# One-hot factors of a gate matrix: two engines write them token by token with scalar compares, in straight code

## The chip, the cores and the metric

The kernel runs on one core of one Trainium2 chip, as one launch. The metric is the device time of that launch in microseconds (us), the median of three runs. Engines are named as the profile names them: PE multiplies matrices, DVE, ACT and POOL work on 128-partition tiles, SP issues the transfers.

## What is computed

Two blocks run one after the other on 256 tokens of width 1024. The first has two layers, each a bank of five mixers and then a feed-forward over product keys (PEER), and the change lies in that feed-forward. The second is a recurrent layer and a gated delta layer, which the change does not touch. The reference of the feed-forward, cut to what matters:

```python
sc = einsum('bshjc,hjkc->bshjk', q, subkeys)            # 8 heads, 2 halves, 128 keys
top_s, top_i = top_k(sc, 16)
best, ci = top_k(top_s[..., 0, :, None] + top_s[..., 1, None, :], 16)
idx = i1 * 128 + i2                                      # i1, i2: keys picked in the two halves
g = softmax(best)
act = gelu(einsum('ckd,cd->ck', u_tab[idx], x))
out = einsum('ck,ckd->cd', g * act, v_tab[idx])
```

Each token picks 8 x 16 = 128 of 128 x 128 experts, each with a gate g. The kernel does not gather the experts. It goes through all of them, 128 at a time, and multiplies by a gate matrix G that holds, for each token, the gate of each expert and zero where it was not picked.

## The kernel before

The loop over two layers (`nc.Fori(0, LAYERS)`) holds one program per engine, tied together by semaphores alone: there is no scheduler, and each engine runs its rows in the order in which they are written. The feed-forward of a layer has four stages.

1. Queries and key scores on PE, top 16 on DVE, and then the slots: per token 128 numbers i1, 128 numbers i2 and 128 gates, which PE transposes (L537) and ACT copies to `slot` (L741), so that a partition is a slot and a column a token.
2. The gate matrix. For each token t the matrix is a product on PE of two 128 x 128 factors: `ha` has in row p a one at column i1 of slot p, times the gate of slot p; `hb` has in row p a one at column i2. Tokens are taken four at a time, 64 groups per layer. DVE makes each factor of a group with one TENSOR_TENSOR over 128 x 512 that compares `iota` (a row 0 to 127) with `slot`, both broadcast (`one_hot`, L1097). POOL multiplies `ha` by the gates in place (`gate_rows`, L841). PE multiplies (`gate_products`, L547), four products into a bank, banks 0 and 1 in turn, and ACT copies the bank to `G` (L748).
3. The experts: 256 chunks from memory through the ring `weight_ring`, split in two parts by ACT (L755) and DVE (L1129), multiplied by PE (L570 and L582).
4. The sum, turned back and added to the token stream.

Around the change the order is set by these semaphores. `first_hot` says that DVE has written a group of `ha`, `first_gated` that POOL has gated it, `second_hot` that `hb` is there, `g_ready` that PE has multiplied a group and `g_kept` that ACT has copied it. There are four buffers for `ha` and two for `hb`, all inside the weight ring (from column WSIZE + D), so SP holds back the expert load number E_HOT and all behind it until the last group is multiplied (L329). Loads 0 and 1 are let through before. PE, DVE and ACT all start stage 3 only behind the last `g_kept` (PE at L559). PE, POOL and DVE run the groups in hardware loops of four groups a turn, ACT in one of two a turn, with the token's column as a register address; the last four groups of DVE are written out.

Of the kernel before, what the change touches and what calls it, by code (L numbers as in the profile page):

```python
# [9 lines left out]
ALU = mybir.AluOpType  # L10
# [82 lines left out]
E_HOT = 2  # L93
assert (N_ALL + E_HOT) % WSLOTS == 2

# [51 lines left out]
def first_block(nc, ctx, mem_, ins):  # L147
# [72 lines left out]
    ha = hot(4, 4, P)  # L220
    hb = hot(2, 4, P)
    GROUPS = T // 4
    ROUND = 4
# [61 lines left out]
    with nc.Fori(0, LAYERS) as l:  # L285
        with nc.Block() as block:

            @block.sync
            def _(sp):
# [36 lines left out]
                for k in range(WSLOTS):  # L326
                    sp.wait_ge(s("w_used"), N_ALL + k - WSLOTS + 1)
                    if k == E_HOT:
                        sp.wait_ge(s("g_ready"), 4 + GROUPS)  # L329
                    sp.dma_start(wring[:, (N_ALL + k) % WSLOTS, 0:D], d_e[l, k]).then_inc(s(f"w_loaded{(N_ALL + k) % WSLOTS}"), 16)  # L330
# [6 lines left out]
            def _(pe):  # L337
# [203 lines left out]
                def gate_products(g, count):  # L541

                    pe.wait_ge(s("first_gated"), count)
                    pe.wait_ge(s("second_hot"), count)
                    pe.wait_ge(s("g_kept"), count)
                    for j in range(4):
                        last = nc.tensor.matmul(nc_ps[g % 2][:, j * P:(j + 1) * P], ha[:, g % 4, j], hb[:, g % 2, j], start=True, stop=True)  # L547
                    last.then_inc(s("g_ready"), 1)

                with pe.Fori(0, GROUPS // ROUND) as i:  # L550
                    for g in range(ROUND):
                        gate_products(g, i * ROUND + (g + 1))


                pe.wait_ge(s("g_kept"), 2 + T // 4)
# [53 lines left out]
            def _(act):  # L609
# [118 lines left out]
                for m in range(2 * PH):  # L728
                    act.wait_ge(s("w_used"), N_WQ + m + 1)
                    nc.scalar.copy(query[:, m], nc_ps[m % 4][:, 0:T]).then_inc(s("query_kept"), 1)  # L730
                    if (m >= 2 and m % 2 == 0) or m == 2 * PH - 1:
# [4 lines left out]
                        nc.scalar.copy(score[:, h % 4], nc_ps[4 + h % 4][:, :].rearrange("p (a c) -> p a c", a=2 * NT)).then_inc(s("score_kept"), 1)  # L736
                act.wait_ge(s("best_shifted"), 1)
# [5 lines left out]
                act.wait_ge(s("slots_kept"), 1)  # L743
                act.sem_inc(s("g_kept"), 2)
                with act.Fori(0, T // 8) as i:
                    for g in range(2):
                        act.wait_ge(s("g_ready"), i * 2 + (g + 5))
                        nc.scalar.copy(G[:, bass.ds(i * 8 + 4 * g, 4)], nc_ps[g][:, :].rearrange("p (a c) -> p a c", a=4)).then_inc(s("g_kept"), 1)  # L748
# [33 lines left out]
            def _(pool):  # L782
# [56 lines left out]
                def gate_rows(g, position, count):  # L839
                    pool.wait_ge(s("first_hot"), count)  # L840
                    nc.gpsimd.tensor_tensor(ha[:, g % 4], ha[:, g % 4], slot[:, 2, bass.ds(position, 4)].unsqueeze(2).broadcast_to([P, 4, P]),  # L841
                                            ALU.mult).then_inc(s("first_gated"), 1)

                with pool.Fori(0, GROUPS // ROUND) as i:
                    for g in range(ROUND):
                        gate_rows(g, i * (4 * ROUND) + 4 * g, i * ROUND + (g + 1))

            @block.vector
            def _(dve):
# [245 lines left out]
                def one_hot(out, half, position, ready):  # L1095

                    nc.vector.tensor_tensor(out, iota.unsqueeze(1).broadcast_to([P, 4, P]),  # L1097
                                            slot[:, half, bass.ds(position, 4)].unsqueeze(2).broadcast_to([P, 4, P]),
                                            ALU.is_equal).then_inc(s(ready), 1)

                dve.sem_inc(s("g_ready"), 4)
                one_hot(ha[:, 0], 0, 0, "first_hot")
                with dve.Fori(0, GROUPS // ROUND - 1) as i:
                    for g in range(ROUND):
                        dve.wait_ge(s("g_ready"), i * ROUND + (g + 2))
# [982 lines left out]
```

## Time and profile before

| what | us |
|---|---|
| median of three runs | 2940.0 (2939.86 to 2942.03) |
| span of the profiled execution | 2947.2 |
| PE busy | 2511.8 (85%) |
| DVE busy | 2067.6 (70%) |
| ACT busy | 1024.6 (35%) |
| POOL busy | 677.2 (23%) |
| L1097, the one-hots on DVE, both layers | 262.3 |
| L841, the gating on POOL, both layers | 169.2 |

The profiled execution is one of its own, and of its time only the span is known. It lies 7.2 us, 0.24%, above the median of the timed runs. The busy figures are sums over the whole span, so that an engine that is fully busy for a short stage and idle for the rest looks idle here; such a stage is read from the rows of its own stretch.

### The profile page before, as it was taken

To read this page: it belongs to the slowest core of one execution; us is meant where nothing else is said; L and a number is where in the kernel's file an instruction comes from. 1 tells how busy PE (TensorE), PEld (TensorE's weight loads), DVE (VectorE), ACT (ScalarE), POOL (GpSimd) and SP (SyncE) were. 2 spreads that over 40 slices of the span, in tenths; PEclk is the share of its full clock that TensorE was granted. 3 is DMA by queue.
4 is the path that set the end of the run, shared out by engine and by line. 5 is a ranking of instruction groups with operands and counts; after the bars stand their busy time and mean duration, and the time that the engine had idled before them with its cause. 6 is when DMAs were issued, how large, how long until landed. Compare 5 with 4: busy or idle time off the path is not lost. (4 is left out here: it accounts for less than half of the span.)

```text
span 2947.2 us, 44691 instructions
## 1 busy us (share of the span) xinstructions
PE 2511.8 (85%) x15512; PEld 2266.9 (77%) x15512; DVE 2067.6 (70%) x3346; ACT 1024.6 (35%) x1572; POOL 677.2 (23%) x548
## 2 busy tenths in 40 slices
PE   7859456999999999987593579999999999768898
PEld 7738346899999999877373468999999998758897
DVE  7585999666666666685769996666666665749652
ACT  4221122444444444342211224444444444444321
POOL 5571256000000000055712560000000000516340
PEclk9769778999999999987697789999999999889898
DMA  5424100555555555453241005555555554424201
GB/s 189 142 72 157 51 0 0 178 186 187 188 187 185 185 186 187 140 188 127 74 161 43 0 0 189 189 186 186 189 187 185 185 185 140 141 87 146 76 1 36
DMA packets 107647, 392.07 MB, mean 133 GB/s; under 512 B 11952, under 2 KB 13360, under 8 KB 107184
## 3 DMA queue, kind: packets, MB, share of 16 engines
q1 hardware_dynamic: 107568, 391.02, 39.4%
q8 instruction: 49, 0.80, 0.1%
q14 instruction: 30, 0.25, 0.0%
HBM read 389.93 MB, written 1.05 MB: 133 GB/s over the span
## 5 line engine op out<-in xcount | busy, mean ns | idle before, releaser
L570 PEld LDWEIGHTS bank<-x_parts,chunk_parts 128*128 128x128 f32 x6144 | 772.0, 192 | 23.1 <-DVE chunk_parts L1129 3.5
L570 PE MATMUL bank<-x_parts,chunk_parts 128*128 128x256 f32 x6144 | 778.5, 283 | 2.5 <-DVE chunk_parts L1129 2.5
L1129 DVE TENSOR_TENSOR chunk_parts<-weight_ring,chunk_parts 128x1024 fp32r<-128x1024 f32 x512 | 625.6, 1223 | 196.3 <-ACT chunk_parts L755 196.3
L582 PE MATMUL bank<-chunk_parts,weight_parts 128*128 128x512 f32 x3072 | 744.7, 391 | 0.6 <-DVE chunk_parts L1129 0.6
L755 ACT CAST chunk_parts<-weight_ring 128x1024 fp32r<-128x1024 f32 x512 | 535.7, 1047 | 359.3 <-PE bank L582 359.3
L582 PEld LDWEIGHTS bank<-chunk_parts,weight_parts 128*128 128x128 f32 x3072 | 560.7, 188 | 106.8 <-issue 0.9
L1121 DVE TENSOR_TENSOR work<-work,big 128x256 f32<-128x256 f32 x256 | 163.0, 637 | 278.7 <-ACT work L759 278.7
L1097 DVE TENSOR_TENSOR weight_ring<-constants,work 128x512 f32<-128x512 f32 x256 | 262.3, 1101 | 4.1 <-ACT work L741 4.1
L759 ACT ACTIVATE work<-bank 128x256 f32<-128x256 f32 x256 | 98.3, 384 | 466.8 <-PE bank L570 466.8
L547 PE MATMUL bank<-weight_ring 128*128 128x128 f32 x1024 | 184.1, 337 | 83.9 <-issue 74.8
L547 PEld LDWEIGHTS bank<-weight_ring 128*128 128x128 f32 x1024 | 160.8, 240 | 107.5 <-issue 98.9
L841 POOL TENSOR_TENSOR weight_ring<-weight_ring,work 128x512 f32<-128x512 f32 x128 | 169.2, 1322 | 119.1 <-DVE weight_ring L1097 119.1
L1411 PE MATMUL bank<-x_parts,chunk_parts 128*128 128x256 f32 x1152 | 153.0, 297 | 25.5 <-POOL chunk_parts L1401 25.5
L785 POOL MEMSET big<- 128x572 f32 x2 | 1.2, 576 | 740.9 <-issue 734.9
L1411 PEld LDWEIGHTS bank<-x_parts,chunk_parts 128*128 128x128 f32 x1152 | 150.2, 205 | 27.5 <-POOL chunk_parts L1401 12.6
L1317 POOL MEMSET big<- 128x24 f32 x1 | 0.1, 123 | 732.3 <-issue 732.3
L748 ACT COPY big<-bank 128x512 f32 x128 | 75.0, 586 | 192.4 <-PE bank L547 192.4
L1401 POOL TENSOR_TENSOR chunk_parts<-weight_ring,chunk_parts 128x1024 fp32r<-128x1024 f32 x48 | 123.3, 2580 | 76.7 <-ACT chunk_parts L1395 76.7
L256 POOL TENSOR_TENSOR big<-big 128x512 f32<-128x512 f32 (+4 forms) x190 | 124.0, 653 | 14.9
L527 PE MATMUL bank<-big,weight_ring 128*128 128x256 f32 x512 | 117.1, 388 | 5.9 <-DVE big L860 5.9
L407 PE MATMUL bank<-x_parts,chunk_parts 128*128 128x256 f32 x768 | 104.8, 299 | 17.1 <-issue 12.0
L253 POOL TENSOR_TENSOR big<-big 128x1024 f32<-128x1024 f32 x38 | 93.1, 2450 | 105.2 <-DMA big<-in_ada 105.2
(355 smaller groups left out, 2812.6 us busy)
## 6 DMA issues: line engine op xcount, KB each, us to landing
weight_ring<-in_experts SPq DMA_DIRECT2D x512, 512.0 KB, 3.3
big<-in_ada SPq DMA_DIRECT2D x48, 512.0 KB, 4.3
weight_ring<-in_w_in SPq DMA_DIRECT2D x40, 512.0 KB, 4.6
weight_ring<-in_wq SPq DMA_DIRECT2D x32, 512.0 KB, 3.2
weight_ring<-in_gdn_in SPq DMA_DIRECT2D x32, 512.0 KB, 3.3
weight_ring<-in_w_out SPq DMA_DIRECT2D x16, 640.0 KB, 4.0
weight_ring<-in_lru_in SPq DMA_DIRECT2D x16, 512.0 KB, 3.3
weight_ring<-in_w_kv SPq DMA_DIRECT2D x8, 512.0 KB, 4.4
```

The source lines that it names most:

```text
L256: link(ops.tensor_tensor(w_[:, 0:width], w_[:, 0:width], w_[:, width:2 * width], ALU.add))
L527: last = nc.tensor.matmul(nc_ps[m % 4][:, 0:T], wt[:, k], xn[:, k], start=(k == 0), stop=(k == KD - 1))
L547: last = nc.tensor.matmul(nc_ps[g % 2][:, j * P:(j + 1) * P], ha[:, g % 4, j], hb[:, g % 2, j], start=True, stop=True)
L570: last = nc.tensor.matmul(nc_ps[2 + n % 2][:, 0:T], a[:, j * P:(j + 1) * P], xr[:, x, j], start=(j == 0 and a is hi and x == 0), stop=(j = ...
L582: last = nc.tensor.matmul(nc_ps[4 + 2 * tt + c][:, 0:512], wr[:, x, n % 2, tt * P:(tt + 1) * P], v[:, c * 512:(c + 1) * 512], start=False, ...
L755: nc.scalar.copy(split[:, k % SPLITS, 0], wring[:, slot_, 0:D]).then_inc(s("hi_done"), 1)
L841: nc.gpsimd.tensor_tensor(ha[:, g % 4], ha[:, g % 4], slot[:, 2, bass.ds(position, 4)].unsqueeze(2).broadcast_to([P, 4, P]), ALU.mult).the ...
L1097: nc.vector.tensor_tensor(out, iota.unsqueeze(1).broadcast_to([P, 4, P]), slot[:, half, bass.ds(position, 4)].unsqueeze(2).broadcast_to([P ...
L1121: nc.vector.tensor_tensor(wgt[:, n % 2], act_e[:, n % 2], G[:, :, bass.ds(tile, 1)].squeeze(2), ALU.mult).then_inc(s("w_full"), 1)
L1129: nc.vector.tensor_tensor(split[:, k % SPLITS, 1], wring[:, (N_ALL + k) % WSLOTS, 0:D], split[:, k % SPLITS, 0].bitcast(F32), ALU.subtract ...
L1401: nc.gpsimd.tensor_tensor(split[:, n % SPLITS, 1], ring[n % R2], split[:, n % SPLITS, 0].bitcast(F32), ALU.subtract).then_inc(s("lo_done"), 1)
L1411: last = nc.tensor.matmul(out, split[:, n % SPLITS, a, k * P:(k + 1) * P], xr[:, x, k], start=(k == 0 and a == 0 and x == 0), stop=(k == K ...
```

## The change

DVE no longer writes `ha`. It writes `hb` alone, with four TENSOR_SCALAR of 128 x 128 per group, one per token, each comparing iota with one column of `slot` as a scalar per partition. Its iota is a copy in PSUM bank 3, which ACT makes once per layer, between the last key scores and the Exp of the gates. POOL writes `ha` from nothing, also with four TENSOR_SCALAR of 128 x 128 per group, which compare iota (in SBUF) with one column of `slot` and multiply by the gate's column. `first_hot` is gone. Both factors have three buffers (HOTS) in place of four and two, in the same space. All loops over groups are written out, so addresses and waits are constants.

```diff
--- before.py
+++ after.py
@@ -91,6 +91,7 @@
 
 NE = 2 * NK
 E_HOT = 2
+HOTS = 3
 assert (N_ALL + E_HOT) % WSLOTS == 2
 
 
@@ -217,10 +218,10 @@
     wgt = w(2, T)
     hot = Region(mem_["wring_"], WSLOTS * WSIZE + P * 2)
     hot.at = WSIZE + D
-    ha = hot(4, 4, P)
-    hb = hot(2, 4, P)
+    ha = hot(HOTS, 4, P)
+    hb = hot(HOTS, 4, P)
     GROUPS = T // 4
-    ROUND = 4
+    iota_ps = nc_ps[3][:, 0:P]
     out_e = big[:, 0:D]
     G = big[:, :].rearrange("p (t k) -> p t k", t=T)
 
@@ -326,7 +327,7 @@
                 for k in range(WSLOTS):
                     sp.wait_ge(s("w_used"), N_ALL + k - WSLOTS + 1)
                     if k == E_HOT:
-                        sp.wait_ge(s("g_ready"), 4 + GROUPS)
+                        sp.wait_ge(s("g_ready"), GROUPS)
                     sp.dma_start(wring[:, (N_ALL + k) % WSLOTS, 0:D], d_e[l, k]).then_inc(s(f"w_loaded{(N_ALL + k) % WSLOTS}"), 16)
                 with sp.Fori(0, NE // WSLOTS - 1) as i:
                     for e in range(WSLOTS):
@@ -538,21 +539,19 @@
                     last.then_inc(s("slots_turned"), 1)
 
 
-                def gate_products(g, count):
-
-                    pe.wait_ge(s("first_gated"), count)
-                    pe.wait_ge(s("second_hot"), count)
-                    pe.wait_ge(s("g_kept"), count)
+                for g in range(GROUPS):
+                    pe.wait_ge(s("first_gated"), g + 1)
+                    pe.wait_ge(s("second_hot"), g + 1)
+                    if g == 0:
+                        pe.wait_ge(s("slots_kept"), 1)
+                    if g >= 2:
+                        pe.wait_ge(s("g_kept"), g - 1)
                     for j in range(4):
-                        last = nc.tensor.matmul(nc_ps[g % 2][:, j * P:(j + 1) * P], ha[:, g % 4, j], hb[:, g % 2, j], start=True, stop=True)
+                        last = nc.tensor.matmul(nc_ps[g % 2][:, j * P:(j + 1) * P], ha[:, g % HOTS, j], hb[:, g % HOTS, j], start=True, stop=True)
                     last.then_inc(s("g_ready"), 1)
 
-                with pe.Fori(0, GROUPS // ROUND) as i:
-                    for g in range(ROUND):
-                        gate_products(g, i * ROUND + (g + 1))
-
-
-                pe.wait_ge(s("g_kept"), 2 + T // 4)
+
+                pe.wait_ge(s("g_kept"), GROUPS)
                 pe.wait_ge(s("zeros"), 1)
                 for tt in range(NT):
                     for c in range(2):
@@ -734,18 +733,17 @@
                         if h >= 4:
                             act.wait_ge(s("score_used"), h - 3)
                         nc.scalar.copy(score[:, h % 4], nc_ps[4 + h % 4][:, :].rearrange("p (a c) -> p a c", a=2 * NT)).then_inc(s("score_kept"), 1)
+                act.wait_ge(s("query_kept"), 2 * PH)
+                nc.scalar.copy(iota_ps, iota).then_inc(s("iota_there"), 1)
                 act.wait_ge(s("best_shifted"), 1)
                 nc.scalar.activation(ex, ex, ACT.Exp).then_inc(s("best_exp"), 1)
                 act.wait_ge(s("slots_turned"), NT)
                 for j in range(3):
                     last = nc.scalar.copy(slot[:, j], nc_ps[j][:, 0:T])
                 last.then_inc(s("slots_kept"), 1)
-                act.wait_ge(s("slots_kept"), 1)
-                act.sem_inc(s("g_kept"), 2)
-                with act.Fori(0, T // 8) as i:
-                    for g in range(2):
-                        act.wait_ge(s("g_ready"), i * 2 + (g + 5))
-                        nc.scalar.copy(G[:, bass.ds(i * 8 + 4 * g, 4)], nc_ps[g][:, :].rearrange("p (a c) -> p a c", a=4)).then_inc(s("g_kept"), 1)
+                for g in range(GROUPS):
+                    act.wait_ge(s("g_ready"), g + 1)
+                    nc.scalar.copy(G[:, 4 * g:4 * g + 4], nc_ps[g % 2][:, :].rearrange("p (a c) -> p a c", a=4)).then_inc(s("g_kept"), 1)
 
 
                 def high(k, slot_, loaded, free):
@@ -836,14 +834,15 @@
                                             ALU.mult).then_inc(s("hit_keyed"), 1)
 
 
-                def gate_rows(g, position, count):
-                    pool.wait_ge(s("first_hot"), count)
-                    nc.gpsimd.tensor_tensor(ha[:, g % 4], ha[:, g % 4], slot[:, 2, bass.ds(position, 4)].unsqueeze(2).broadcast_to([P, 4, P]),
-                                            ALU.mult).then_inc(s("first_gated"), 1)
-
-                with pool.Fori(0, GROUPS // ROUND) as i:
-                    for g in range(ROUND):
-                        gate_rows(g, i * (4 * ROUND) + 4 * g, i * ROUND + (g + 1))
+                pool.wait_ge(s("slots_kept"), 1)
+                pool.wait_ge(s("w_used"), N_ALL)
+                for g in range(GROUPS):
+                    if g >= HOTS:
+                        pool.wait_ge(s("g_ready"), g - HOTS + 1)
+                    for j in range(4):
+                        t = 4 * g + j
+                        last = nc.gpsimd.tensor_scalar(ha[:, g % HOTS, j], iota, slot[:, 0, t:t + 1], slot[:, 2, t:t + 1], ALU.is_equal, ALU.mult)
+                    last.then_inc(s("first_gated"), 1)
 
             @block.vector
             def _(dve):
@@ -1092,27 +1091,15 @@
                 dve.wait_ge(s("slots_kept"), 1)
                 dve.wait_ge(s("w_used"), N_ALL)
 
-                def one_hot(out, half, position, ready):
-
-                    nc.vector.tensor_tensor(out, iota.unsqueeze(1).broadcast_to([P, 4, P]),
-                                            slot[:, half, bass.ds(position, 4)].unsqueeze(2).broadcast_to([P, 4, P]),
-                                            ALU.is_equal).then_inc(s(ready), 1)
-
-                dve.sem_inc(s("g_ready"), 4)
-                one_hot(ha[:, 0], 0, 0, "first_hot")
-                with dve.Fori(0, GROUPS // ROUND - 1) as i:
-                    for g in range(ROUND):
-                        dve.wait_ge(s("g_ready"), i * ROUND + (g + 2))
-                        one_hot(ha[:, (g + 1) % 4], 0, i * (4 * ROUND) + 4 * (g + 1), "first_hot")
-                        dve.wait_ge(s("g_ready"), i * ROUND + (g + 3))
-                        one_hot(hb[:, g % 2], 1, i * (4 * ROUND) + 4 * g, "second_hot")
-                for g in range(GROUPS - ROUND, GROUPS):
-                    if g + 1 < GROUPS:
-                        dve.wait_ge(s("g_ready"), g + 2)
-                        one_hot(ha[:, (g + 1) % 4], 0, 4 * (g + 1), "first_hot")
-                    dve.wait_ge(s("g_ready"), g + 3)
-                    one_hot(hb[:, g % 2], 1, 4 * g, "second_hot")
-                dve.wait_ge(s("g_kept"), 2 + T // 4)
+                dve.wait_ge(s("iota_there"), 1)
+                for g in range(GROUPS):
+                    if g >= HOTS:
+                        dve.wait_ge(s("g_ready"), g - HOTS + 1)
+                    for j in range(4):
+                        t = 4 * g + j
+                        last = nc.vector.tensor_scalar(hb[:, g % HOTS, j], iota_ps, slot[:, 1, t:t + 1], None, ALU.is_equal)
+                    last.then_inc(s("second_hot"), 1)
+                dve.wait_ge(s("g_kept"), GROUPS)
```

Here is how the rows of two engines stand. First DVE from the last reduction of the slots to the first split of stage 3. `weight_ring` is where `ha` and `hb` lie, `work` holds `slot`, `constants` holds iota, `bank` is PSUM, and `m_` stands before each semaphore's name. Before, within the loop:

```order
363 L1087 TENSOR_REDUCE big<-big 128x128 [waits m_hit_keyed]
364 L1097 TENSOR_TENSOR weight_ring<-constants,work 128x512 [waits m_w_used,m_slots_ready,m_slots_kept]
365 L1103 UNCONDITIONAL_BRANCH
366 L1103 ISA
367 L1097 ISA [waits m_g_ready]
368 L1097 TENSOR_TENSOR weight_ring<-constants,work 128x512
369 L1107 REGISTER_ALU
370 L1097 ISA [waits m_g_ready]
371 L1097 TENSOR_TENSOR weight_ring<-constants,work 128x512
```

And with the change:

```order
363 L1086 TENSOR_REDUCE big<-big 128x128 [waits m_hit_keyed]
364 L1100 TENSOR_SCALAR weight_ring<-bank,work 128x128 [waits m_w_used,m_iota_there,m_slots_kept,m_slots_ready]
365 L1100 TENSOR_SCALAR weight_ring<-bank,work 128x128 x11
366 L1100 TENSOR_SCALAR weight_ring<-bank,work 128x128 [waits m_g_ready]
367 L1100 TENSOR_SCALAR weight_ring<-bank,work 128x128 x3
```

Three groups (12 instructions) run before the first wait for PE, and then one wait stands before each group of four.

Second, POOL after the last multiplication of the slots' stage. Before:

```order
164 L835 TENSOR_TENSOR big<-big 128x2048 [waits m_hit_ready] x3
165 L844 UNCONDITIONAL_BRANCH
166 L844 ISA
167 L841 ISA [waits m_first_hot]
168 L841 TENSOR_TENSOR weight_ring<-weight_ring,work 128x512
169 L840 REGISTER_ALU
```

And with the change:

```order
164 L833 TENSOR_TENSOR big<-big 128x2048 [waits m_hit_ready] x3
165 L844 TENSOR_SCALAR weight_ring<-constants,work 128x128 [waits m_w_used,m_slots_kept]
166 L844 TENSOR_SCALAR weight_ring<-constants,work 128x128 x11
167 L844 TENSOR_SCALAR weight_ring<-constants,work 128x128 [waits m_g_ready]
168 L844 TENSOR_SCALAR weight_ring<-constants,work 128x128 x3
```

POOL no longer waits for DVE. It waits for ACT's copy of the slots, and then for PE alone.

## Rows read from the trace of the kernel before

**Rows 1.** The page: busy time, share of the span and instructions of each engine.
```profile
PE 2511.8 (85%) x15512; PEld 2266.9 (77%) x15512; DVE 2067.6 (70%) x3346; ACT 1024.6 (35%) x1572; POOL 677.2 (23%) x548
```

**Rows 2.** Windows, both gate stages: busy us (instructions) of each engine, PEclk, DMA.
```profile
core 0: us, PE busy (x) PEld busy (x) DVE busy (x) ACT busy (x) POOL busy (x), PEclk, DMA share, GB/s
388.50:522.00 133.50, 91.85 (x512) 80.23 (x512) 131.15 (x128) 36.93 (x63) 84.60 (x64) 0.82 0.00 0
1638.50:1771.00 132.50, 92.20 (x512) 80.53 (x512) 131.16 (x128) 36.94 (x63) 84.59 (x64) 0.82 0.00 0
```

**Rows 3.** Timeline, start of both gate stages: start, us, what [idle before <-releaser].
```profile
387.49 0.92 ACT L741 COPY work<-bank 128x256 f32<-128x256 f32 x3 [31.61 <-PE bank L537]
388.55 4.19 DVE L1097 TENSOR_TENSOR weight_ring<-constants,work 128x512 f32<-128x512 f32 x4 [2.05 <-ACT work L741]
389.44 2.75 POOL L841 TENSOR_TENSOR weight_ring<-weight_ring,work 128x512 f32<-128x512 f32 x2 [14.45 <-DVE weight_ring L1097]
...
1637.52 0.92 ACT L741 COPY work<-bank 128x256 f32<-128x256 f32 x3 [31.61 <-PE bank L537]
```

**Rows 4.** Timeline, inside the first gate stage.
```profile
439.75 16.46 DVE L1097 TENSOR_TENSOR weight_ring<-constants,work 128x512 f32<-128x512 f32 x16
...
446.17 1.30 POOL L841 TENSOR_TENSOR weight_ring<-weight_ring,work 128x512 f32<-128x512 f32 x1 [0.74 <-DVE weight_ring L1097]
...
446.68 1.87 PE L547 MATMUL bank<-weight_ring 128*128 128x128 f32 x8 [0.92 <-issue]
448.20 1.33 POOL L841 TENSOR_TENSOR weight_ring<-weight_ring,work 128x512 f32<-128x512 f32 x1 [0.72 <-DVE weight_ring L1097]
...
448.55 1.52 DVE L1097 TENSOR_TENSOR weight_ring<-constants,work 128x512 f32<-128x512 f32 x1
...
450.00 0.68 DVE L1097 TENSOR_TENSOR weight_ring<-constants,work 128x512 f32<-128x512 f32 x1
...
450.73 0.59 ACT L748 COPY big<-bank 128x512 f32 x1 [1.46 <-PE bank L547]
```

**Rows 5.** Timeline, end of both gate stages.
```profile
522.71 1.04 PE L559 MATMUL bank<-constants,zeros 128*128 128x512 bf16 x4 [0.77 <-ACT big L748]
...
1767.86 1.33 POOL L841 TENSOR_TENSOR weight_ring<-weight_ring,work 128x512 f32<-128x512 f32 x1 [0.72 <-DVE weight_ring L1097]
...
1769.83 1.13 PE L547 MATMUL bank<-weight_ring 128*128 128x128 f32 x8 [0.32 <-issue]
1771.10 0.59 ACT L748 COPY big<-bank 128x512 f32 x1 [0.86 <-PE bank L547]
...
1771.74 0.61 PE L559 MATMUL bank<-constants,zeros 128*128 128x512 bf16 x2 [0.77 <-ACT big L748]
```

**Rows 6.** Line L1097 on DVE: ns min/median/max, first and last start us, forms.
```profile
L1097 DVE TENSOR_TENSOR weight_ring<-constants,work x256: 676/1106/1530, 388.5 to 1768.2; 128x512 f32<-128x512 f32 x128
```

**Rows 7.** Timeline, DVE in the delta layer: 16 scalar instructions reading PSUM.
```profile
2780.78 4.23 DVE L1843 TENSOR_SCALAR big<-bank,work 128x128 f32<-128x128 f32 x16
```

**Rows 8.** POOL's groups by shape: busy us, mean ns.
```profile
L256 POOL TENSOR_TENSOR big<-big 128x128 f32<-128x128 f32 x38 | 19.6, 515 | 3.0
...
L258 POOL TENSOR_TENSOR big<-big 128x16 f32<-128x16 f32 x38 | 9.3, 244 | 3.0
...
L796 POOL COPY big<-big 128x512 f32<-128x512 f32 x2 | 1.2, 620 | 4.4 <-ACT big L658 4.4
...
L801 POOL COPY big<-big 64x256 f32<-64x256 f32 x2 | 0.8, 392 | 0.1
...
L1317 POOL MEMSET big<- 128x24 f32 x1 | 0.1, 123 | 732.3 <-issue 732.3
```

**Rows 9.** Timeline, POOL: two copies in a row, no wait between them.
```profile
42.35 0.39 POOL L801 COPY big<-big 64x256 f32<-64x256 f32 x1
42.79 0.40 POOL L802 COPY big<-big 64x256 f32<-64x256 f32 x1
```

## The prediction

> **What bounds the kernel now.** I read the page first. PE is busy for 85% of the span and DVE for 70% [rows 1], which says little about a stage that fills 9% of it. So I read the windows of the two gate stages [rows 2]. In 133.5 us DVE is busy for 131.15, ACT for 37, POOL for 85 and PE for 92. DVE is the bound there, and nothing else is near. The DMA share is 0.00, since the expert loads wait for the stage's end, so no transfer can be the bound inside it.
>
> Next, the pace. In the timeline DVE does 16 instructions in 16.46 us without a gap [rows 4], two per group, so a group takes 2.06 us, and 64 groups take 131.7. The two are far from equal. The one that starts at 450.00 has POOL idle beside it and takes 0.68 us; the one at 448.55 runs beside POOL's multiplication (448.20 to 449.53), takes 1.52, and the next starts only 1.45 later [rows 4]. All 256 lie between 676 and 1530 ns [rows 6]. The inference is that DVE's compare, with two inputs in SBUF, loses about 0.8 us per group to POOL.
>
> Last, the edges of the stage. It begins when ACT has copied the slots (387.49 + 0.92 = 388.41, and 1638.44 in the second layer) [rows 3] and ends when PE starts L559 (522.71 and 1771.74) [rows 5]. So it is 134.3 us long in the first layer and 133.3 in the second. All engines stand at both edges, so a microsecond saved inside is a microsecond of the kernel, twice. The rest of the program is the same, so the whole change is in these 267.6 us.
>
> **The change part by part.** With P the pace of a group, the new stage is: 0.15 us from the slots to the first compare (388.41 to 388.55 [rows 3]), then 64 P until the last factor is there, 0.1 until PE starts, and from there to L559 what rows 5 show, 1771.74 - 1769.83 = 1.9. So it is 64 P + 2.2 us, and today's pace is matched at P = (133.8 - 2.2) / 64 = 2.06. P is the largest of four costs.
>
> DVE. 256 wide compares leave the program, and per group four TENSOR_SCALAR of 128 x 128 come, with iota in PSUM and the scalar in `work`. The trace has just this form: 16 of them take 4.23 us, 0.26 each from start to start [rows 7]. A group costs 4 x 0.26 = 1.06 us, half of now. The compares of `ha` leave DVE altogether.
>
> PE. The same 256 products per layer. They keep PE busy for 91.85 us [rows 2], 1.44 us per group, because the granted clock is 0.82 of full, changing between its two levels, 2.4 and 1.2 GHz: a group takes 1.13 us at the higher [rows 5] and 1.87 where much of it fell to the lower [rows 4]. PE's floor is 1.13 if the clock is full all through, and 1.44 as it is granted now. Above a pace of 1.44, three buffers take up a slow group.
>
> ACT. 64 copies of 0.59 us [rows 5] per layer, as before. Two banks go round: product 1.13 to 1.87, copy 0.59 and two handovers of some 0.15 come to 2.0 to 2.8 us per two groups, 1.0 to 1.4 per group, no more than PE. The new copy of iota to PSUM is one small instruction per layer and stands before the Exp. ACT sat idle for 31.6 us before it copied the slots [rows 3], which covers it; without this cover it would cost less than the 0.59 of a copy four times as wide. It waits only for queries that ACT itself copied, so nothing queues up behind it.
>
> POOL. It did one multiplication per group and now does four TENSOR_SCALAR, each with a compare, a product and two scalars per partition. The trace has no such instruction on POOL. Call X its time from start to start, so that P = 4 X. Bound below: a copy reads one tensor and writes one. Two in a row start 0.44 us apart at 256 elements [rows 9]. From 392 ns at 256 to 620 at 512 elements [rows 8] an element costs 0.89 ns, so a copy of 128 would take 0.44 - 0.11 = 0.32. A compare with scalars is not cheaper than a copy, except that start-to-start times may overlap, and I keep 0.28 as the lower end. Bound above: I take the TENSOR_TENSOR of 128 x 128, 515 ns [rows 8], which reads twice as much, and beyond it the case of the rivals. The value I take is nearest to the copy, plus the fetch of the scalars. What a read costs POOL shows between a write alone, 123 ns (memset, 24 elements), and a short read and write, 244 ns (16 elements) [rows 8]: 0.12 us. With one such fetch, X = 0.32 + 0.12 = 0.44 and P = 1.76. No row of the trace gives the second arithmetic operation a cost, and I take none.
>
> Loops. 57 ns register steps and branches go, but they are hidden under DVE's instructions, as DVE has no gap [rows 4]. Straight code has more instructions to fetch. The unrolled parts of the same program run without a gap of the kind in L1843's sixteen [rows 7]; nothing is charged, and a microsecond or two per layer is within the range. The waits: POOL may be three groups ahead of PE, so its wait for group g - 3 is over long before (1.76 + 1.2 + 0.3 us of work against 5.3 us of lead). SP's wait for the last group ends with the stage, as now, and the loads behind it move with it.
>
> **The sum.** POOL sets the pace: 64 x 1.76 + 2.2 = 114.8 us per layer. That is 19.5 less in the first and 18.5 less in the second, 38.0 together. The profiled execution goes from 2947.2 to 2909.2. It lies 7.2 above the median, which I carry over: **2902 us**. PE, at 1.44 of 1.76, is next.
>
> **The rivals.** A measurement of this kernel can tell about 0.2%, 5.9 us, from no change; that is X within 0.012 of 0.514.
>
> *POOL is cheaper, PE is the bound.* If X is 0.36 or less, PE's clock decides. For it speaks that both inputs of the work are small; against it, that the copy alone already costs 0.32. At 1.44 the stage is 94.4 us, 78.8 less in all: 2861. At a full clock (1.13, X under 0.28) it would be 74.5 us: 2821.
>
> *Each scalar is a fetch of its own: slower.* The place is POOL's instruction, before its stream starts. Two fetches of 0.12 give X = 0.32 + 0.24 = 0.56 and P = 2.24, a stage of 145.6 us, 23.6 more in all: 2964. It decides from X = 0.514 upwards. For it: the short instructions on POOL all look like fixed cost, 244 ns for 16 elements [rows 8]. Against: the addresses of both scalars are known at once and may be fetched together. The Trainium skill has a rule for it (GPSIMD Engine Reference, Performance pitfalls for Q7 kernels): a small read command costs about 102 cycles and does not overlap with the one before. By its figure at 1.2 GHz, an estimate of 85 ns each, X would be 0.49 and the time 2928; no row here shows such a command by itself. A compare that costs more per element than a copy would lead to the same place: 0.9 ns more for each of 128 elements is another 0.12.
>
> *The scalars cost about what the split saves.* X within 0.012 of 0.514, which is also the TENSOR_TENSOR's 515 ns: no change, 2940.
>
> *DVE and POOL still get in each other's way.* The wide compares lose some 0.8 us per group beside POOL [rows 4]. If the narrow ones exclude POOL's, a group takes 4 x (0.26 + 0.44) = 2.8 us, and the time is 2940 + 2 x 181.4 - 267.6 = 3035. Rows 7 say nothing about it, as POOL stood still there. Against it: the iota that DVE reads is not in SBUF, so only one operand, the scalar, comes from there. The Trainium skill (SBUF — State Buffer, Who interferes with whom) says that a DVE instruction with at most one SBUF input and outside the 2-port modes does not contend with GpSimd. The trace agrees in the other half, that two SBUF inputs do (1.52 us against 0.68); the half that counts here no row shows.
>
> **How the numbers follow.** POOL sets the pace with X from 0.36 to 0.50: 0.46. PE is the bound: 0.22. No change: 0.07. Slower through the fetches or the compare: 0.21. Contention: 0.04. So faster 0.68, same 0.07, slower 0.25. The likeliest case's own range is X from 0.36 to 0.50, 64 x 1.44 + 2.2 = 94.4 to 64 x 2.0 + 2.2 = 130.2 us per layer, 2861 to 2933. To leave out no more than 2 in 10, the range goes down to where PE has a clock somewhat better than now (P about 1.32, 86.7 us, 2846) and up to X = 0.59 (153.2 us, 2979).
>
> **What the new profile would show.** DVE's instructions near 0.26 us from start to start, and DVE idle, waiting for PE, for about 40% of the stage. POOL without a gap, four instructions in 1.76 us. PE waiting for POOL before each group, and no POOL waiting for DVE. The stage's start and its end 115 us apart. The forecast is wrong if POOL waits for PE (then PE was the bound and X is small), if four POOL instructions take more than 2.06 us, if DVE's take more than 0.26 only while POOL runs, or if the time outside the two stages moves.

## The result: 140 us slower

The changed kernel takes 3080.2 us (median of four runs, 3074.4 to 3085.4) against 2939.9 for the kernel before. The ratio is 1.0475, with a 95% interval from 1.0459 to 1.0492. I had forecast 2902, with a range from 2846 to 2979.

The page of the changed kernel, its share of busy time (as rows 1 before) and the group that answers to L841 and L1097:

```profile
PE 2590.3 (84%) x15510; PEld 2332.1 (76%) x15512; DVE 1947.7 (63%) x3602; ACT 1024.7 (33%) x1574; POOL 903.1 (29%) x932
...
L844 POOL TENSOR_SCALAR weight_ring<-constants,work 128x128 f32<-128x128 f32 x512 | 396.0, 791 | 27.1 <-ACT work L742 27.1
```

POOL's 512 instructions take 396.0 us in all. POOL is busy for only 29% of the span, and yet it is the engine that sets the time, because all of these lie in two stages in which everything waits for it. The windows of the two stages, as rows 2 showed them before:

```profile
core 0: us, PE busy (x) PEld busy (x) DVE busy (x) ACT busy (x) POOL busy (x), PEclk, DMA share, GB/s
388.30:589.00 200.70, 132.81 (x512) 113.93 (x512) 71.84 (x256) 37.29 (x65) 198.00 (x256) 0.50 0.00 0
1703.00:1904.00 201.00, 132.75 (x512) 113.93 (x512) 71.85 (x256) 37.59 (x66) 198.00 (x256) 0.50 0.00 0
```

POOL is busy for 198.0 of 200.7 us. DVE went from 131 to 72 us of busy time, as intended, and now idles. PE is granted 0.50 of its clock throughout, 1.2 GHz, against 0.82 before, and does the same 512 records. The timeline of a stretch inside, and the edges of both stages (start us, us, engine, line; in brackets the idle time before):

```profile
387.42 0.92 ACT L742 COPY work<-bank 128x256 f32<-128x256 f32 x3 [31.61 <-PE bank L538]
...
439.50 8.52 POOL L844 TENSOR_SCALAR weight_ring<-constants,work 128x128 f32<-128x128 f32 x11
...
441.12 2.08 PE L550 MATMUL bank<-weight_ring 128*128 128x128 f32 x8 [1.02 <-POOL weight_ring L844]
443.23 0.58 ACT L746 COPY big<-bank 128x512 f32<-128x512 f32 x1 [2.52 <-PE bank L550]
443.23 1.13 DVE L1100 TENSOR_SCALAR weight_ring<-bank,work 128x128 f32<-128x128 f32 x4 [1.97 <-PE bank L550]
444.21 2.07 PE L550 MATMUL bank<-weight_ring 128*128 128x128 f32 x8 [1.01 <-POOL weight_ring L844]
...
589.65 1.49 PE L558 MATMUL bank<-constants,zeros 128*128 128x512 bf16 x3 [1.08 <-ACT big L746]
...
1702.47 0.92 ACT L742 COPY work<-bank 128x256 f32<-128x256 f32 x3 [31.61 <-PE bank L538]
...
1904.70 1.49 PE L558 MATMUL bank<-constants,zeros 128*128 128x512 bf16 x3 [1.08 <-ACT big L746]
```

Eleven POOL instructions take 8.52 us without a gap, so one starts (8.52 - 0.79) / 10 = 0.773 us after the other, and a group takes 3.09 us. DVE's four take 1.13 us and then wait 1.97 for PE to free a buffer. PE waits 1.0 us for POOL before each group. The stage is 589.65 - 388.34 = 201.3 us long, and as long in the second layer (1904.70 - 1703.39). Against 134.3 and 133.3 before, that is 135.0 us more. The spans differ by 3081.2 - 2947.2 = 134.0. So the whole loss is in the two stages; the medians differ by 140.3, since the profiled execution of before lay 7 us above its median and this one 1 us above its own.

### The profile page after: what moved, and what is told of

Same layout as the page of the kernel before. It is cut to its first block and busy times, and to the rows that moved or that the text cites. A ratio compares the mean times of both kernels' runs of the same rounds, so it can differ in the third digit from the quotient of the medians.

```text
span 3081.2 us, 43977 instructions
## 1 busy us (share of the span) xinstructions
PE 2590.3 (84%) x15510; PEld 2332.1 (76%) x15512; DVE 1947.7 (63%) x3602; ACT 1024.7 (33%) x1574; POOL 903.1 (29%) x932
## 5 line engine op out<-in xcount | busy, mean ns | idle before, releaser
L844 POOL TENSOR_SCALAR weight_ring<-constants,work 128x128 f32<-128x128 f32 x512 | 396.0, 791 | 27.1 <-ACT work L742 27.1
L550 PE MATMUL bank<-weight_ring 128*128 128x128 f32 x1024 | 265.6, 441 | 136.8 <-POOL weight_ring L844 128.3
L550 PEld LDWEIGHTS bank<-weight_ring 128*128 128x128 f32 x1024 | 227.9, 328 | 174.7 <-POOL weight_ring L844 174.7
L1100 DVE TENSOR_SCALAR weight_ring<-bank,work 128x128 f32<-128x128 f32 x512 | 143.7, 344 | 244.4 <-PE bank L550 240.4
L746 ACT COPY big<-bank 128x512 f32<-128x512 f32 x128 | 74.9, 585 | 326.8 <-PE bank L550 326.8
```

Of the source, the lines that this page charges most:

```text
L844: last = nc.gpsimd.tensor_scalar(ha[:, g % HOTS, j], iota, slot[:, 0, t:t + 1], slot[:, 2, t:t + 1], ALU.is_equal, ALU.mult)
L1100: last = nc.vector.tensor_scalar(hb[:, g % HOTS, j], iota_ps, slot[:, 1, t:t + 1], None, ALU.is_equal)
```

## The experiments

After the result the question was what makes POOL's instruction 0.773 us long, where I had taken 0.44. Three theories: each **scalar** costs a fixed fetch; the **arithmetic** costs per element; or DVE beside it causes **contention**. Beside them stood the parts of the change that I had costed at nothing. Each ratio below is against runs of the kernel before that were timed along with the variant (medians 2943.2 and 2942.8 us). The two tails were run once each, for the lengths of their instructions alone.

**Forms of the instruction, measured by themselves.** A tail is code behind the last layer, in which nothing else runs. Parts of it (`...` marks what is left out here):

```diff
+            for i in range(6):
+                g.tensor_copy(new(), iota)
...
+            for i in range(6):
+                g.tensor_scalar(new(), iota, s0, s1, ALU.mult, ALU.add)
+            for i in range(6):
+                g.tensor_scalar(new(), iota, s0, s1, ALU.is_equal, ALU.mult)
...
+            for i in range(24):
+                g.tensor_scalar(new(), iota, s0, s1, ALU.is_equal, ALU.mult)
+        @block.vector
+        def _(dve):
+            for i in range(64):
+                nc.vector.tensor_scalar(new(), m["ps"][3][:, 0:P], s0, None, ALU.is_equal)
```

> The kernel before, with a tail behind its last layer, in which nothing else runs, that does six to 24 POOL instructions of each form in a row, each to a place of its own, and then some of DVE. It is for the time from start to start of one instruction; the kernel's time grows by the tail and says nothing. The changed kernel showed 0.773 us for POOL's compare-and-multiply of 128 x 128 with two scalars from memory. Theory of the fetch (each scalar costs a fixed read, the stream runs like a copy): a copy 0.3, immediates in place of the scalars 0.3 to 0.35, one scalar 0.55, two 0.77 whatever the operation; 384 elements with two scalars 0.77 + 0.23 = 1.0; 32 elements 0.69. Theory of the element (the arithmetic costs per element, the scalars nothing): immediates 0.77 as with scalars, one operation clearly under two, 384 elements about 2.0, 32 elements about 0.35. Theory of contention (DVE beside it slows POOL): 0.45 alone in every form, and 0.77 only in the block where DVE runs beside it reading PSUM. In the block where DVE reads iota from SBUF instead, all theories expect both engines slower than alone, if the two ports matter. DVE alone from SBUF: about 0.19 to 0.20 from start to start against 0.26 from PSUM.

The lines of the tail, one form each (ns min/median/max of one, start of the first and the last). L1982 is a copy; L1986 an equality with an immediate, L1990 with one scalar; L1992 multiply and add with two immediates, L1994 equality and multiply with two immediates; L1996 and L1998 the same pairs with two scalars; L2000 and L2002 are L1998 at 32 and 384 elements:

```profile
L1982 POOL COPY big<-constants x6: 290/292/293, 2942.7 to 2943.9; 128x128 f32<-128x128 f32 x6
...
L1986 POOL TENSOR_SCALAR big<-constants x6: 529/532/543, 2947.2 to 2949.7; 128x128 f32<-128x128 f32 x6
...
L1990 POOL TENSOR_SCALAR big<-constants x6: 616/618/619, 2953.7 to 2956.6; 128x128 f32<-128x128 f32 x6
L1992 POOL TENSOR_SCALAR big<-constants x6: 318/320/323, 2957.2 to 2958.5; 128x128 f32<-128x128 f32 x6
L1994 POOL TENSOR_SCALAR big<-constants x6: 667/668/672, 2958.7 to 2961.8; 128x128 f32<-128x128 f32 x6
L1996 POOL TENSOR_SCALAR big<-constants x6: 471/482/486, 2962.4 to 2964.6; 128x128 f32<-128x128 f32 x6
L1998 POOL TENSOR_SCALAR big<-constants x6: 831/834/841, 2965.0 to 2968.9; 128x128 f32<-128x128 f32 x6
L2000 POOL TENSOR_SCALAR big<-constants x6: 521/525/528, 2969.6 to 2971.9; 128x32 f32<-128x32 f32 x6
L2002 POOL TENSOR_SCALAR big<-constants x6: 1703/1708/1714, 2972.3 to 2980.4; 128x384 f32<-128x384 f32 x6
```

Three readings. First, a scalar costs 618 - 532 = 86 ns, and two cost 834 - 668 = 166 in one pair and 482 - 320 = 162 in the other: two cost twice what one does, 0.083 us each, as if each were fetched by itself. Second, with two immediates multiply-add takes 320 ns, hardly more than a copy's 292, and equality-multiply 668. The pair of operations is worth 0.35 us at 128 elements, with the scalars the same. From start to start, taken from the trace, the same four forms (L1992, L1994, L1996, L1998) lie 0.26, 0.61, 0.43 and 0.77 us apart, with the same differences to 0.01 us, so these are not an effect of how the profile ends an instruction. Third, it grows with the width: from 128 to 384 elements equality-multiply gains 874 ns, 3.4 per element, where rows 8 gave 0.89 for a copy. Neither of the first two theories holds alone: above a copy's 0.24 us from start to start lie 0.54, of which the two scalars are 0.17 and the choice of operations 0.35; the rest, about 0.03, is what multiply-add takes above a copy.

And the block with DVE beside it (L2016 POOL, L2020 DVE from PSUM; L2026 POOL, L2030 DVE from SBUF; L2026 stands twice, the second time for the window in which DVE ran, 3018.1 to 3032.0 us), then DVE alone from SBUF with one operation (L2036), with two (L2038) and from PSUM with two (L2040):

```profile
L2016 POOL TENSOR_SCALAR big<-constants x24: 787/808/825, 2999.2 to 3016.9; 128x128 f32<-128x128 f32 x24
L2020 DVE TENSOR_SCALAR big<-bank,constants x64: 337/339/350, 2999.1 to 3015.4; 128x128 f32<-128x128 f32 x64
L2026 POOL TENSOR_SCALAR big<-constants x24: 787/908/1026, 3018.1 to 3038.1; 128x128 f32<-128x128 f32 x24
L2026 POOL TENSOR_SCALAR big<-constants x16: 843/910/1026, 3018.1 to 3031.8; 128x128 f32<-128x128 f32 x16
L2030 DVE TENSOR_SCALAR big<-constants x64: 271/281/396, 3018.1 to 3032.0; 128x128 f32<-128x128 f32 x64
L2036 DVE TENSOR_SCALAR big<-constants x16: 280/280/286, 3039.2 to 3042.1; 128x128 f32<-128x128 f32 x16
L2038 DVE TENSOR_SCALAR big<-constants x16: 333/336/342, 3042.3 to 3046.2; 128x128 f32<-128x128 f32 x16
L2040 DVE TENSOR_SCALAR big<-bank,constants x16: 396/396/399, 3046.4 to 3051.2; 128x128 f32<-128x128 f32 x16
```

From start to start POOL takes (3016.9 - 2999.2) / 23 = 0.77 us with DVE beside it reading PSUM, and (2968.9 - 2965.0) / 5 = 0.78 alone. The contention theory falls. With iota in SBUF, POOL's time rises to 20.0 / 23 = 0.87 and DVE's from 2.9 / 15 = 0.19 to 13.9 / 63 = 0.22. But the 0.87 mixes two stretches: as long as DVE ran, POOL's instructions started (3031.8 - 3018.1) / 15 = 0.91 us apart, and behind it 0.77 again. So beside such a DVE an instruction of POOL costs 0.14 us more.

**Straight code alone.** The kernel before, with its loops written out:

```diff
-                with pool.Fori(0, GROUPS // ROUND) as i:
-                    for g in range(ROUND):
-                        gate_rows(g, i * (4 * ROUND) + 4 * g, i * ROUND + (g + 1))
+                for g in range(GROUPS):
+                    gate_rows(g, 4 * g, g + 1)
```

(and so on PE, ACT and DVE).

> The kernel before with the loops over groups of PE, ACT, POOL and DVE written out, nothing else changed: the part of the change that is only straight code. Theory that POOL's new instruction costs all: no change, ratio 1.000, the stage stays at 133 to 134 us. Rival, that straight code itself costs (instruction fetches): the stage grows by up to the 68 us per layer that the change lost.

Measured: 2942.1 us, ratio 0.9994, interval 0.9984 to 1.0003. In its profile the two stages are 134.3 and 133.2 us long, as before. Straight code is neither the loss nor a gain.

**Which pairs are slow.** A second tail, with other pairs of operations, all with two scalars from memory:

> The kernel before with a second tail behind its last layer: POOL's TENSOR_SCALAR of 128 x 128 with two scalars from memory and other pairs of operations, six of each. Measured before: multiply then add 0.44 us from start to start, compare then multiply 0.78, a single multiply 0.58. If comparing is what is slow, all pairs without a compare take 0.44 (multiply-multiply, multiply-subtract, add-multiply, subtract-multiply, max-multiply) and equal-add and greater-multiply 0.78. If instead one pair alone, multiply-add, runs on a quick path and all others go through a general one, every other pair takes about 0.78, and at 384 elements multiply-multiply takes 1.64 as compare-multiply did, against about 0.8 for multiply-add. Output in bf16 in place of fp32: no change in either case.

L1980 is multiply-multiply, L1982 multiply-subtract, L1984 add-multiply, L1988 equality-add, L1992 max-multiply; L1996 is multiply-multiply at 384 elements:

```profile
L1980 POOL TENSOR_SCALAR big<-constants x6: 447/447/451, 2944.7 to 2946.9; 128x128 f32<-128x128 f32 x6
L1982 POOL TENSOR_SCALAR big<-constants x6: 792/792/816, 2947.3 to 2951.2; 128x128 f32<-128x128 f32 x6
L1984 POOL TENSOR_SCALAR big<-constants x6: 447/447/448, 2952.0 to 2954.1; 128x128 f32<-128x128 f32 x6
...
L1988 POOL TENSOR_SCALAR big<-constants x6: 791/791/816, 2959.2 to 2963.1; 128x128 f32<-128x128 f32 x6
...
L1992 POOL TENSOR_SCALAR big<-constants x6: 787/788/794, 2968.5 to 2972.4; 128x128 f32<-128x128 f32 x6
...
L1996 POOL TENSOR_SCALAR big<-constants x6: 660/660/661, 2977.0 to 2980.2; 128x384 f32<-128x384 f32 x6
```

Both guesses miss. The quick ones are pairs of multiply and add; a subtraction is as slow as a compare, at 792 ns, and the two pairs not shown (subtract-multiply, greater-multiply) take 792 and 791. What the edge is made of can't be seen from here; it may be a general routine behind a few special ones, which was not tested. At 384 elements multiply-multiply takes 660 ns, 0.83 per element more than at 128, where equality-multiply had 3.4. The output in bf16 took 791 ns as well. The profile's length of one form differs a little from place to place (834 ns in the first tail, 791 in the changed kernel); from start to start it is 0.77 us in both.

**The changed kernel with a quick pair.** One edit. The first factor is then no one-hot, so the gate matrix, and what comes behind it, holds other values; the work is the same in number and size.

```diff
-                        last = nc.gpsimd.tensor_scalar(ha[:, g % HOTS, j], iota, slot[:, 0, t:t + 1], slot[:, 2, t:t + 1], ALU.is_equal, ALU.mult)
+                        last = nc.gpsimd.tensor_scalar(ha[:, g % HOTS, j], iota, slot[:, 0, t:t + 1], slot[:, 2, t:t + 1], ALU.mult, ALU.add)
```

> The changed kernel, but POOL's instruction multiplies by its first scalar and adds its second in place of comparing and multiplying: same width, same two scalars from memory, another pair of operations. The first factor is then no one-hot, so the gate matrix and all behind it hold other values. In the tail measured before, this form took 0.44 us from start to start against 0.78. If the pair of operations is what the forecast of 0.44 us lacked, POOL has 1.76 us per group, the stage is 64 x 1.76 + 2.2 = 115 us as forecast, and the time 2940 - 38 = 2902, perhaps 5 more or less. If something else in the stage held the changed kernel (the waits, straight code, PE at its lower level with 2.07 us per group), the time stays at 2940 or above.

Measured: 2901.1 us, ratio 0.9862 (0.9843 to 0.9880). The windows from 400 to 480 us, and POOL's and DVE's groups in them:

```profile
400.00:480.00 80.00, 53.84 (x373) 45.00 (x373) 52.79 (x188) 27.50 (x47) 80.00 (x188) 1.00 0.00 1
...
L844 POOL TENSOR_SCALAR weight_ring<-constants,work 128x128 f32<-128x128 f32 x188 | 80.6, 443 | 0.0
L1100 DVE TENSOR_SCALAR weight_ring<-bank,work 128x128 f32<-128x128 f32 x188 | 52.9, 344 | 27.7 <-PE bank L550 27.7
```

188 of POOL's instructions in 80 us are 0.43 us each and 1.70 per group. Everything else in the stage is as the change has it: the waits, straight code, three buffers, DVE reading PSUM. With the instruction at about the length of the forecast, the kernel runs at about the time of the forecast. One price carries the error.

**DVE alone, from PSUM and from SBUF.** POOL is taken out, and DVE writes both factors; in the second kernel `iota` stands in both of its rows for `iota_ps`, and ACT's copy of iota is gone. PE no longer waits for `first_gated`. The lines added for `ha`:

```diff
+                    for j in range(0, 4):
+                        t = 4 * g + j
+                        nc.vector.tensor_scalar(ha[:, g % HOTS, j], iota_ps, slot[:, 0, t:t + 1], slot[:, 2, t:t + 1], ALU.is_equal, ALU.mult)
```

> DVE writes both factors as in the run with iota in SBUF, but reads iota from PSUM as the change does. In the tail DVE took 0.26 us for one operation and 0.32 for two with two scalars, both from PSUM, so 4 x 0.26 + 4 x 0.32 = 2.32 us per group, a stage of about 151 us and a time of about 2940 + 2 x 151 - 268 = 2974. If PSUM cost nothing, it would be 2912 as with SBUF.

> The changed kernel with POOL out of the stage: DVE writes both factors, eight narrow instructions per group, with iota read from SBUF. If the narrow form from SBUF takes 0.19 to 0.20 us from start to start (by the 341 ns that 256 elements from SBUF and 128 from PSUM both take), the pace is 1.55 to 1.6 and the time about 2880. If it takes 0.26 as from PSUM, the pace is 2.08 and the time 2940 to 2945. PE's clock could hold either at 2.07 per group.

From PSUM 2977.5 us (two runs; 1.0121, 1.0089 to 1.0153), close to the 2974 expected; from SBUF 2911.9 (0.9895, 0.9878 to 0.9911). The second was expected near 2880: the pace is 4 x 0.19 for `hb` and 4 x 0.26 for `ha`, 1.81 us, because the second operation and its scalar cost DVE another 0.06 us each, which L2038 against L2036 shows and which I had not known then. Reading iota from SBUF makes DVE's instruction shorter by 0.06 us; the change paid that for freedom from POOL. And DVE alone, without POOL's help, is 1.0% faster than the kernel before.

**The change with iota in SBUF.**

```diff
-                        last = nc.vector.tensor_scalar(hb[:, g % HOTS, j], iota_ps, slot[:, 1, t:t + 1], None, ALU.is_equal)
+                        last = nc.vector.tensor_scalar(hb[:, g % HOTS, j], iota, slot[:, 1, t:t + 1], None, ALU.is_equal)
```

> The changed kernel with DVE's iota in SBUF, which lets DVE use both ports. In the tail POOL's compare-and-multiply took 0.87 us from start to start while DVE's narrow compares ran without pause beside it, and 0.77 alone. Here DVE is busy for only a quarter of the time, so if the ports matter in proportion POOL goes to 0.79 to 0.80 and the time to 3085 to 3095. If they do not matter, 3080.

Measured: 3095.6 us (two runs; 1.0522, 1.0497 to 1.0548), at the upper end of what was expected. POOL's mean went from 791 to 820 ns, and its group from 3.09 to 3.22 us (PE starts groups at 439.43, 442.65 and 445.88). So the copy in PSUM was right for this division of the work: by the two ratios, 1.0522 and 1.0475, it is worth about 14 us. The two stages of the profile, 209.3 and 209.4 us against 201.3, give 16. The group grew by 0.13 us, about what one of its four POOL instructions costs more beside DVE in the tail (0.14).

**The work divided evenly.** POOL writes the first factor of two tokens in four, DVE that of the others and all second factors:

```diff
-                    for j in range(4):
+                    for j in range(2):
                         t = 4 * g + j
                         last = nc.gpsimd.tensor_scalar(ha[:, g % HOTS, j], iota, slot[:, 0, t:t + 1], slot[:, 2, t:t + 1], ALU.is_equal, ALU.mult)
...
+                    for j in range(2, 4):
+                        t = 4 * g + j
+                        nc.vector.tensor_scalar(ha[:, g % HOTS, j], iota_ps, slot[:, 0, t:t + 1], slot[:, 2, t:t + 1], ALU.is_equal, ALU.mult)
```

> The changed kernel, but POOL writes the first factor of two tokens of each group and DVE that of the other two beside its second factor, so POOL has two instructions per group and DVE six. If POOL's instruction costs 0.773 us wherever it stands, POOL has 1.55 us per group and DVE 6 x 0.26 = 1.56: a pace of 1.56 to 1.6, a stage of about 103 us, 2940 - 2 x 31 = about 2880. If contention with DVE made it 0.773, more DVE work makes it longer: a pace above 1.6 with POOL's instruction above 0.8. If PE is granted its lower level all the time, as in the changed kernel (2.07 us per group), PE sets the pace at about 2.07 and the time stays near 2940.

> As split_two (POOL two first factors of each group, DVE the other two and all second factors), but DVE's first factors read iota from SBUF, where its form with two operations took 0.26 us against 0.32 from PSUM in the tail. DVE: 4 x 0.26 + 2 x 0.26 = 1.56 us per group in place of 1.68, POOL 1.55 and a little more where the two-port instructions meet it. If both hold, a pace of about 1.6 and 2 x 64 x 0.07 = 9 us less than split_two, about 2882. If the ports cost POOL 0.1 us or more per instruction, POOL has 1.75 and it is slower than split_two.

The first took 2891.1 us, ratio 0.9827 (0.9811 to 0.9844): DVE needs 4 x 0.26 + 2 x 0.32 = 1.68 per group, not 1.56, and sets the pace (from 400 to 480 us it is busy for all 80 us, POOL for 75.6). The second took 2888.0, ratio 0.9816 (0.9797 to 0.9835). Its groups from 400 to 480 us:

```profile
400.00:480.00 80.00, 58.39 (x405) 48.67 (x403) 80.00 (x304) 29.43 (x51) 80.00 (x102) 1.00 0.00 1
...
L844 POOL TENSOR_SCALAR weight_ring<-constants,work 128x128 f32<-128x128 f32 x102 | 81.0, 809 | 0.0
L1103 DVE TENSOR_SCALAR weight_ring<-bank,work 128x128 f32<-128x128 f32 x202 | 56.3, 336 | 0.0
L1100 DVE TENSOR_SCALAR weight_ring<-constants,work 128x128 f32<-128x128 f32 x102 | 32.1, 353 | 0.0
```

POOL and DVE are both busy for all 80 us: 102 POOL instructions are 51 groups, 1.57 us each. The two kernels are 52 and 55 us faster than the kernel before, and some 190 faster than the changed one. The step from the first to the second was to bring 9 us and brought 3, and the two intervals overlap. In the profiles the stage fell from 109.0 to 104.1 us in the first layer and to 106.1 in the second, 8 us together, while the work ahead of the first, the same in both, happened to take 3 us longer (ACT's copy of the slots began at 385.0 against 382.1).

## Why the prediction was wrong

**The bound and the places** were right. DVE was the bound of the stage, both stages were the whole field of the change, and what was lost lies inside them (135.0 us in the stages, 134.0 in the whole span).

**DVE** at 0.26 us per instruction and 1.06 per group was right (4 in 1.13 us with the last one's tail). Rows 7 held the very form.

**The step that failed is POOL's price**, "X = 0.32 + 0.12 = 0.44 and P = 1.76". It was built from the copy plus one fetch, with the sentence "No row of the trace gives the second arithmetic operation a cost, and I take none". Measured: X = 0.773 and P = 3.09. The term takes apart as follows. The copy from start to start is (2943.9 - 2942.7) / 5 = 0.24, less than my 0.32. The two scalars cost 0.17 in place of 0.12, and multiply-add 0.03 more than a copy. And the pair equality-multiply costs 0.35 more than multiply-add, in place of nothing. The small errors cancel, by luck: 0.43 us is measured for multiply-add with two scalars. My 0.12 for one fetch was also misread: the 244 ns are those of a TENSOR_TENSOR, which reads two tensors, so the row gave 0.06 for each. So the operations are the whole miss: (0.773 - 0.44) x 4 x 64 x 2 = 170 us of the 178 between the forecast and the result. Most of the rest is the offset of 7.2 us between the profiled execution and the median, which I had carried over from before and which was 1.0 after the change.

**The formula** 64 P + 2.2 held. With 3.094 it gives 200.2 against 201.3 measured, and most of the 1.1 us left is the last product, 2.07 us at PE's lower level in place of 1.13. With the 1.70 of muladd_form it gives 111.0 us, and both stages there took 111.8 (the first from 388.4 to 500.2). That is 3 us less than the 114.8 of the forecast, so that its 2901.1, next to 2902, is a closer hit than the terms are: by its ratio it would be 2899 where the kernel before takes 2939.9.

**The bounds** were the other error. I took the TENSOR_TENSOR of 128 x 128 (515 ns) as the bound above, because it reads twice as much. That is a bound for reading, and the instruction's time was set by which operations it does (not by how many: a single multiplication took 529 ns, multiply-add 320). No row of the trace before spoke of a compare on POOL; for such a price the range should have been open above, and the rival's chance of 0.21 larger.

**The rivals.** The slow rival had the mechanism in part: each scalar costs by itself, at 0.083 us. The Trainium skill's rule (GPSIMD Engine Reference, Performance pitfalls for Q7 kernels), about 102 cycles per small read that does not overlap, gives an estimate of 85 ns at the 1.2 GHz that the page states. The measured 83 ns agree; that a scalar is fetched by such a read is inferred from this number alone. With two scalars at 0.083, and nothing for the operations, X would have been 0.49 and the kernel near 2928, still faster than before. It also named a compare that costs more per element, with 0.9 ns for it; it is nearer 2.5. The cheap-POOL rival did not happen. Contention did not either: 0.77 us beside DVE against 0.78 alone, the same within the rounding. The rule of the Trainium skill that I had cited for it (SBUF — State Buffer, Who interferes with whom), that a DVE instruction with at most one SBUF input and outside the 2-port modes does not contend, agrees with these two numbers. With iota in SBUF, POOL loses 0.14 us beside a DVE that never pauses; whether DVE is then in a 2-port mode no row says, but its own instruction is shorter (0.19 us against 0.26).

**PE's clock** I had taken over from the kernel before, with 1.44 us for the products of a group. It followed the pace: 0.82 before, 0.50 in the changed kernel, 1.00 in the windows of the runs with a pace of 1.6 to 1.7. At 0.50 a group took 2.07 us, which a pace of 3.09 still hides. So the clock cost only the last product.

**Edits costed at nothing** were rightly so: straight code (0.9994), ACT's copy of iota (L737, 0.28 us at 327.46, in ACT's idle time) and the waits (muladd_form).

## What to carry to other kernels

An instruction that the trace does not show on an engine has two unknowns, what it reads and what it computes, and a neighbour that bounds the one does not bound the other; where 512 of them would set the pace, twenty lines at the end of the kernel measure it before anything is redesigned. When two engines share a stage, divide by measured prices until both are full: the idea of the change was sound and gained 1.7 to 1.8% once POOL had two of eight instructions instead of four. And look at the busy share of the stage, not of the kernel: POOL set the time here at 29% of the span.

## What was not expected of the hardware

- On POOL, TENSOR_SCALAR of 128 x 128 fp32 takes 443 to 482 ns with two scalars when both operations are multiplications or additions (three pairs tried), and 788 to 834 ns with a subtraction, a maximum or a compare among them (six pairs tried). A single multiplication with an immediate (529 ns, L1984 of the first tail) is slower than multiply-add with two (320 ns):

```profile
L1984 POOL TENSOR_SCALAR big<-constants x6: 528/529/548, 2944.3 to 2946.8; 128x128 f32<-128x128 f32 x6
```

- Each scalar from memory costs POOL 0.083 us, and two cost twice that. On DVE one operation more with its scalar costs 0.06 us (L2038 against L2036).
- PE's granted clock fell from 0.82 to 0.50 when the pace went from 2.06 to 3.09 us per group, was 0.74 at 2.32 (DVE alone from PSUM) and 1.00 at 1.6 to 1.8, all in windows from 400 to 480 us or the whole stage. PE had the same products to do each time. In these runs, the slower it was fed, the slower its clock; it did not matter here only because the feeder was slower still. The windows of DVE alone, from PSUM and then from SBUF:

```profile
400.00:480.00 80.00, 56.51 (x279) 48.45 (x280) 80.00 (x278) 20.06 (x35) 0.00 (x0) 0.74 0.00 1
400.00:480.00 80.00, 51.36 (x358) 42.95 (x356) 80.00 (x355) 25.79 (x44) 0.00 (x0) 1.00 0.00 1
```
